# A hybrid decoder step on one core: shorter routing chain, thinned layer-norm sums, and pooling products evicted by ScalarE

## The reference

```
h = rmsnorm(x) ; p = h @ w_in                    # columns: conv value | conv gate | pool input
a = v * sigmoid(gate); y = depthwise_conv31(a)   # 1024 channels
yc = silu(layernorm(y + b_dw))                   # mean and variance over the 1024 channels
s = trailing_mean(u) - u                         # windows 2, 4, 8, 16 for 4 groups of 256
yp = (s @ w_pool[g]) * pool_scale
x = x + concat(yc, yp) @ w_out
h2 = rmsnorm(x); group = argmax(h2 @ w_rg); two best of its 8 experts by h2 @ w_re
x = x + sum_e gate_e * (silu(h2 @ w_gate[e]) * (h2 @ w_up[e])) @ w_down[e]   # 32 experts, width 512
y = rmsnorm(x)
```

## Time and profile before

| what | value |
|---|---|
| median of 3 runs | 1390.73 us (1390.59 to 1391.2) |
| profiled execution, its own time | 1391.43 us |
| its span, first to last instruction | 1389.6 us |
| granted TensorE clock, mean | 0.974 |
| PE busy | 1281.5 us (92%) |
| DVE busy | 344.3 us (25%) |
| ACT busy | 101.4 us (7%) |
| POOL busy | 102.4 us (7%) |
| data moved | 464.61 MB, mean 334 GB/s |

### The profile page before, as it was taken

The page is one execution under the profiler, slowest core; times in us unless marked ns, Lnnn a source line. Parts: engine busy times, 40 slices in busy tenths (PEclk is TensorE's granted clock), DMA queues, the critical chain, the costliest instruction groups (busy, mean ns, idle before and its releaser), DMA issues.

```text
span 1389.6 us, 16405 instructions
## 1 busy us (share of the span) xinstructions
PE 1281.5 (92%) x6548; PEld 721.1 (52%) x6548; DVE 344.3 (25%) x699; ACT 101.4 (7%) x232; POOL 102.4 (7%) x164
## 2 busy tenths in 40 slices
PE   9999989999999998989998989899889989889876
PEld 7777767777865443444343445444344444334321
DVE  4499933011342110101101011110101101010226
ACT  2100012000100000000000000000000000000012
POOL 2211152000000000000000000000000000000000
PEclk9999999999999999999999999999999999999997
DMA  9444325565439999999999999999999999999894
GB/s 237 165 143 158 122 67 170 199 243 211 166 138 372 426 426 427 428 430 425 428 426 426 428 427 427 427 425 428 421 427 422 418 427 419 428 426 410 341 321 118
DMA packets 82486, 464.61 MB, mean 334 GB/s; under 512 B 8079, under 2 KB 50191, under 8 KB 56195
## 3 DMA queue, kind: packets, MB, share of 16 engines
q1 hardware_dynamic: 76784, 455.89, 81.3%
q0 software_dynamic: 5392, 7.86, 1.8%
q10 hardware_dynamic: 283, 0.48, 0.1%
HBM read 456.67 MB, written 20.80 MB: 344 GB/s over the span
## 4 chain that ended last, share of the span: by engine, by line
PE 44%; DMA 41%; issue 7%; DVE 5%; SPq 1%; ACT 0%; DVEq 0%; ACTq 0%
DMA arena<-in_w_up_dram 41%; PE bank L716 21%; PE bank L562 14%; PE bank L737 3%; DVE arena L979 3%; PE bank L694 2%; SPq L394 1%; PE bank L788 1%; PE bank L629 1%; PE bank L646 0%; PE bank L599 0%; PE bank L511 0%; PE bank L643 0%; PE bank L791 0%; DVE arena L985 0%
## 5 line engine op out<-in xcount | busy, mean ns | idle before, releaser
L716 PE MATMUL bank<-arena,stage 128*64 128x512 f32 x1920 | 442.8, 615 | 58.3 <-DMA arena<-in_w_up_dram 58.3
L716 PEld LDWEIGHTS bank<-arena,stage 128*64 128x64 f32 x1920 | 146.0, 142 | 347.6 <-issue 304.7
L562 PE MATMUL bank<-arena,stage 128*128 128x288 f32 x1280 | 315.0, 407 | 0.8 <-DVE arena L962 0.8
L562 PEld LDWEIGHTS bank<-arena,stage 128*128 128x128 f32 x1280 | 241.9, 190 | 66.3 <-issue 0.9
L694 PEld LDWEIGHTS bank<-x1w,x1r 96*128 96x128 f32 x1536 | 174.0, 192 | 26.0 <-issue 26.0
L694 PE MATMUL bank<-x1w,x1r 96*128 96x128 f32 x1536 | 180.2, 277 | 0.0
L1222 DVE TENSOR_TENSOR a_sb<-sl_sb,bank 128x256 f32<-128x256 f32 x32 | 19.3, 604 | 498.1 <-ACT sl_sb L895 498.1
L737 PE MATMUL bank<-arena,aT 128*64 128x512 f32 x512 | 113.4, 595 | 8.5 <-ACT aT L897 8.5
L979 DVE SCALAR_TENSOR_TENSOR arena<-arena,wdw 128x256 f32<-128x256 f32 x240 | 103.0, 503 | 0.0
L1359 POOL DMA_INDIRECT expert_rows<-ysb,cur_d x31 | 30.3, 978 | 855.9 <-DVE ysb L1236 827.8
L1236 DVE TENSOR_SCALAR ysb<-bank,wslot 128x512 f32<-128x512 f32 x31 | 23.3, 751 | 255.6 <-PE bank L737 255.6
(11 more groups left out here) (232 smaller groups left out, 483.8 us busy)
## 6 DMA issues: line engine op xcount, KB each, us to landing
arena<-in_w_gate_dram SPq DMA_DIRECT2D x48, 2048.0 KB, 13.7
arena<-in_w_up_dram SPq DMA_DIRECT2D x48, 2048.0 KB, 21.1
arena<-in_w_down_dram SPq DMA_DIRECT2D x30, 2048.0 KB, 17.9
xT<-in_w_down_dram SPq DMA_DIRECT2D x15, 2048.0 KB, 20.4
stage<-in_w_down_dram SPq DMA_DIRECT2D x15, 2048.0 KB, 21.7
arena<-in_w_gate_dram SPq DMA_DIRECT2D x16, 1536.0 KB, 14.8
arena<-in_w_up_dram SPq DMA_DIRECT2D x16, 1536.0 KB, 21.1
stage<-in_w_in_dram SPq DMA_DIRECT2D x11, 2048.0 KB, 8.2
```

What stands on the lines that cost most here:

```text
L562: last = pe.matmul(ps[bank][:, 0:NTOK], wsl[a][:, k, cc * P:(cc + 1) * P], rhs[:, k, :], start=(n == 0), stop=(n == KT - 1))
L716: mm = pe.matmul(ps[4 + s][BLK * h:BLK * (h + 1), :], xgT[:, k, BLK * s:BLK * (s + 1)], w[:, :, 256 * h:256 * (h + 1)], start=(k == 0), st ...
```

## The change

- The 8-tile channel sums are thinned: VectorE first adds tiles to two (for the sum: 8 to 4 to 2; for the squares the same), PE then multiplies only two. The sum's matmuls move behind `pool_inputs(2)`, those of the squares behind `pool_inputs(3)`.
- The state transposes of the pooling rows go to banks 2 and 3, the pool products to banks 4 and 5; ScalarE evicts the products, ahead of the Silus, and then loads the Silu table by a dummy activation. `pool_line(6)` and `(7)` move ahead.
- PE waits for all eight evictions before the projection; the first dense takes the pooled half first and then waits for the convolution half.
- The last group's row squares are split: columns of tiles 0 to 2, then tile 3, before whose transposes PE waits for the first squares. The Sqrt table is loaded ahead. ScalarE, not VectorE, copies the last rows.
- `one_hot(0)` is six comparisons of 128 elements that multiply by the inverse root in the same instruction, and one addition.
- Dummies: 30 and 12 instead of 40 and 18. In the first pair, selections 2 and 3 come after the second gate/up quarter.

```diff
-AWAKE_ROUTE = (40, 18)
+AWAKE_ROUTE = (30, 12)
...
+            def channel_sum(bank, parts):
+
+                for j in range(2):
+                    last = pe.matmul(ps[bank][:, 0:NTOK], ones[:, :], parts[:, j, :], start=(j == 0), stop=(j == 1))
+                return last
...
-            pe.wait_ge(conv_chain, 4 * PERC)
-            for j in range(CT):
-                last = pe.matmul(ps[4][:, 0:NTOK], ones[:, :], yc[:, j, :], start=(j == 0), stop=(j == CT - 1))
-            last.then_inc(sum_mm, 1)
             pool_inputs(2)
+            pe.wait_ge(sum_ready, 1)
+            channel_sum(4, sqw[:, 4:6, :]).then_inc(sum_mm, 1)
+            pool_inputs(3)
             pe.wait_ge(sq_ready, 1)
-            for j in range(CT):
-                last = pe.matmul(ps[5][:, 0:NTOK], ones[:, :], sqw[:, j, :], start=(j == 0), stop=(j == CT - 1))
-            last.then_inc(sumsq_mm, 1)
-            pool_inputs(3)
+            channel_sum(5, sqw[:, 0:2, :]).then_inc(sumsq_mm, 1)
...
-                    last = pe.matmul(ps[6 + i % 2][:, 0:NTOK], wsl[0][:, 2 * g + a, dd * P:(dd + 1) * P], sT[:, 2 * g + a, :],
+                    last = pe.matmul(ps[4 + i % 2][:, 0:NTOK], wsl[0][:, 2 * g + a, dd * P:(dd + 1) * P], sT[:, 2 * g + a, :],
...
-            pe.wait_ge(st_ready, 4)
-            pe.wait_ge(mix_ready, CT)
-            pe.wait_ge(wrs_ready, 1)
-            pe.wait_ge(var_ready, 1)
+            pe.wait_ge(wp_ready, CT)
+            pooled_first = tuple(range(CT, KT)) + tuple(range(CT))
...
-                    dense(q % 2, a, q % 2, mixT, late=(wp_ready, CT) if first and q == 0 else None).then_inc(o_mm, 1)
+                    if first and q == 0:
+                        dense(q % 2, a, q % 2, mixT, order=pooled_first, late=(mix_ready, CT)).then_inc(o_mm, 1)
...
                     elif first:
+                        pe.wait_ge(st_ready, 4)
+                        pe.wait_ge(wrs_ready, 1)
...
+            pe.wait_ge(act_chain, 4 * TT)
             rows_and_router(3, 3)
...
-                            for b in ((0, 1), (2,), (3,), ())[c]:
+                            for b in ((0, 1), (), (2, 3), ())[c]:
...
+            for i in range(CT):
+                act.wait_ge(wp_mm, i + 1)
+                j = CT - 2 - 2 * (i // 2) + i % 2
+                act.activation(mixT[:, CT + j, :], ps[4 + i % 2][:, 0:NTOK], ACT.Copy, scale=pps[:, j:j + 1]).then_inc(wp_ready, 1)
+            act.activation(silu_table[:, :], ones[:, 0:1], ACT.Silu)
...
+            with act.Fori(0, 3) as o:
+                row_squares(o, 0, 4, o)
+            row_squares(3, 0, 3, 3)
+            row_squares(3, 3, 4, 4)
             act.wait_ge(act_in, 2)
             act.activation(sq[:, :], va[:, :], ACT.Sqrt).then_inc(sqrt_done, 1)
+            for t in range(TT):
+                act.copy(x1p[:, t, 96:128, :], ps[2 + t][0:TR, :].rearrange("r (p k) -> r p k", k=KT)).then_inc(row_evac, 1)
...
+            dve.wait_ge(conv_chain, 4 * PERC)
+            dve.tensor_tensor(sqw[:, 0:4, :], yc[:, 0:4, :], yc[:, 4:8, :], ALU.add).then_inc(half_sum, 1)
+            dve.wait_ge(half_sum, 1)
+            dve.tensor_tensor(sqw[:, 4:6, :], sqw[:, 0:2, :], sqw[:, 2:4, :], ALU.add).then_inc(sum_ready, 1)
             dve.wait_ge(nmean_ready, 1)
...
+            dve.wait_ge(squared, 1)
+            dve.tensor_tensor(sqw[:, 0:4, :], sqw[:, 0:4, :], sqw[:, 4:8, :], ALU.add).then_inc(half_sq, 1)
+            dve.wait_ge(half_sq, 1)
+            dve.tensor_tensor(sqw[:, 0:2, :], sqw[:, 0:2, :], sqw[:, 2:4, :], ALU.add).then_inc(sq_ready, 1)
...
-            rows(3)
...
+                if isinstance(m, int) and m == 0:
+                    for c, dst in ((0, hot0), (1, hot)):
+                        for t in range(TT):
+                            ins = dve.tensor_scalar(dst[:, t, :], iof[:, 0:P], slot[:, c, t:t + 1], rs[:, t:t + 1], ALU.is_equal, ALU.mult)
+                        ins.then_inc(hot_chain, 1)
+                    dve.wait_ge(hot_chain, 2)
+                    dve.tensor_tensor(hot, hot, hot0, ALU.add).then_inc(hot_ready, 1)
```

More of the change, by code:

```diff
@@ L141, in hybrid_decoder_step @@
         a_sb = sb("a_sb", [P, 256])
+        silu_table = sb("silu_table", [P, 1])
         sl_sb = sb("sl_sb", [P, 256])
@@ L144, in hybrid_decoder_step @@
         ss = sb("ss", [TR, TT])
-        ssp = sb("ssp", [TR, TT * 4])
+        ssp = sb("ssp", [TR, TT * 5])
+        preload = sb("preload", [TR, 1])
         va = sb("va", [TR, TT])
@@ L312, in hybrid_decoder_step @@
         sqrt_done = sem("sqrt_done")
+        squared = sem("squared")
         nmean_ready = sem("nmean_ready")
@@ L330, in hybrid_decoder_step @@
         centred = sem("centred")
+        half_sum = sem("half_sum")
+        sum_ready = sem("sum_ready")
+        half_sq = sem("half_sq")
         var_ready = sem("var_ready")
@@ L617, in _ @@
                 for j in range(4 * b, 4 * b + 4):
-                    last = pe.transpose(ps[b][0:UK, (j % 4) * P:(j % 4 + 1) * P], uk[:, j, :], ident[:, :])
+                    last = pe.transpose(ps[2 + b][0:UK, (j % 4) * P:(j % 4 + 1) * P], uk[:, j, :], ident[:, :])
                 last.then_inc(st_mm, 1)
             pe.wait_ge(slot_in[0], 16 * 7)
-            pe.wait_ge(st_ready, 2)
+            pe.wait_ge(nmean_ready, 1)
+            pe.wait_ge(var_ready, 1)
             for i in range(CT):
@@ L653, in projection @@
                         pe.wait_ge(slot_in[a], 16 * o + (16 * 7 if a else 16 * 8))
-                    dense(q % 2, a, q % 2, mixT, late=(wp_ready, CT) if first and q == 0 else None).then_inc(o_mm, 1)
+                    if first and q == 0:
+                        dense(q % 2, a, q % 2, mixT, order=pooled_first, late=(mix_ready, CT)).then_inc(o_mm, 1)
+                    else:
+                        dense(q % 2, a, q % 2, mixT).then_inc(o_mm, 1)
                     if q:
@@ L848, in pool_line @@
                          ps[c][:, SEQ:NTOK].rearrange("p (s t) -> p s t", s=NSEQ)).then_inc(u_evac[c // 2], 1)
-            for n in range(4):
+            for n in range(6):
                 pool_line(n)
@@ L854, in _ @@
             act.wait_ge(centred, 1)
[L855 to L858, removed]
+            act.activation(words(arena, O_AW, CT * NTOK), words(arena, O_YC, CT * NTOK), ACT.Square).then_inc(squared, 1)
+            pool_line(6)
+            pool_line(7)
             act.wait_ge(var_ready, 1)
             act.activation(lnr[:, :], lnv[:, :], ACT.Sqrt).then_inc(sqrt_done, 1)
-            pool_line(6)
+            for i in range(CT):
[3 more added lines that the diff above has]
+            act.activation(silu_table[:, :], ones[:, 0:1], ACT.Silu)
             act.wait_ge(yn_ready, 1)
@@ L864, in _ @@
                 act.activation(mixT[:, j, :], yc[:, j, :], ACT.Silu, bias=plb[:, j:j + 1], scale=plg[:, j:j + 1]).then_inc(mix_ready, 1)
-            pool_line(7)
-            for n, (b, r) in enumerate(((6, AK), (7, AK), (0, UK), (1, UK))):
+            for n, (b, r) in enumerate(((6, AK), (7, AK), (2, UK), (3, UK))):
                 act.wait_ge(st_mm, n + 1)
@@ L874, in _, with row_squares @@
             act.dma_start(pool_s[0, :, HP - SLEN:HP, :], strow[HP:UK, 1, :]).then_inc(st_out, 16)
-            with act.Fori(0, 4) as o:
-                act.wait_ge(row_mm, 4 * o + 4)
+            act.activation(preload[:, :], ones[0:TR, 0:1], ACT.Sqrt)
+            def row_squares(o, q0, q1, col):
+                act.wait_ge(row_mm, 4 * o + q1)
                 for t in range(TT):
-                    act.activation(ysb[0:TR, t % 2, (t // 2) * 512:(t // 2 + 1) * 512], ps[2 + t][0:TR, :], ACT.Square,
-                                   accum_out=dyn(ssp, 4 * t + o, 1, TR)).then_inc(act_chain, 1)
+                    act.activation(ysb[0:TR, t % 2, (t // 2) * 512 + q0 * P:(t // 2) * 512 + q1 * P], ps[2 + t][0:TR, q0 * P:q1 * P], ACT.Square,
+                                   accum_out=dyn(ssp, 5 * t + col, 1, TR)).then_inc(act_chain, 1)
+            with act.Fori(0, 3) as o:
+                row_squares(o, 0, 4, o)
+            row_squares(3, 0, 3, 3)
+            row_squares(3, 3, 4, 4)
             act.wait_ge(act_in, 2)
             act.activation(sq[:, :], va[:, :], ACT.Sqrt).then_inc(sqrt_done, 1)
+            for t in range(TT):
+                act.copy(x1p[:, t, 96:128, :], ps[2 + t][0:TR, :].rearrange("r (p k) -> r p k", k=KT)).then_inc(row_evac, 1)
             act.wait_ge(act_in, 3)
@@ L1006, in _ @@
             last.then_inc(wrs_ready, 1)
[L1008 to L1011, removed]
             dve.sem_inc(row_evac, 1)
@@ L1029, in _ @@
             residual(3)
-            dve.wait_ge(act_chain, 4 * TT)
+            dve.wait_ge(act_chain, 5 * TT)
             link(dve.tensor_reduce(ss[:, :], ssp3, AXX, ALU.add))
             dve.tensor_scalar(va[:, :], ss[:, :], 1.0 / D, EPS, ALU.mult, ALU.add).then_inc(act_in, 1)
-            rows(3)
             dve.wait_ge(act_in, 2)
@@ L1085, in one_hot @@
                     dve.wait_ge(key_ready, m)
```

(6 more changed lines are left out.)

1 line of the change is left out of this document (removed).

## The result

| | before | after |
|---|---|---|
| median | 1390.66 us (4 runs) | 1379.14 us (1378.88 to 1379.88, 4 runs) |
| ratio after/before | | 0.992 (95%: 0.9908 to 0.9932) |
| profiled execution / span | 1391.43 / 1389.6 us | 1379.88 / 1378.1 us |

Faster by 11.5 us where 16.4 were forecast: 1379.14 lies just above the range of 1371 to 1379. The way was right, the size was not.

The account below looks back on a forecast made before the run. The expert-weight DMA stream bounds the second half, so it must start earlier: 11.9 us before the second dense plus 4.5 in routing, 16.4 off 1391.43, gives 1375.0 (median 1374.3); range 1372 to 1377, with rivals (1) and (2) 1371 to 1379.

Parts of the forecast that it names:

- GpSimd's last group: Last pooling sums and differences before the projection: 4.6 us from 210.9, ready at 215.6, before PE asks at 218.9.
- the mix wait: PE's wait within the first dense, after its pooled half, for ScalarE's Silus of the convolution half: 1.8 us.
- the routing: Last rows, one-hot and dummies up to the first selection: selection starts 4.5 us earlier, bounds 4.1 to 4.8.
- carrying over: Microseconds saved before the load of the sixth `gu_used` (440.02 us) reach the end one to one.
- The two additions: VectorE's thinning before each channel sum: 2.1 us, at most 2.5 for the first pair, hidden from PE.
- the wait and the sums: PE before the projection: 6.29 us of convolution wait, 5.12 of sums and 2.91 of squares saved, 14.3 together.
- the wait for the last one: PE's new wait before the first dense for ScalarE's last eviction of pool products: 0.6 us lost.
- leaving a drain out of the sum: ScalarE's Silu table switch counted without the skill's drain of some 1380 ns; with it the result would be 1375.7.
- One-hot: Before the first selection: six instructions at 0.21 us and one addition take 1.9 us, against 2.20 before.
- Rival (1): PE's clock falls in the routing after a new 1.2 us wait, slowing the dummies: 1375.7 to 1377 us; chance 0.17.
- Rivals (3): In the expert stage the weight stream starts earlier but PE cannot follow it, up to 1396 us; chance 0.04.
- (4): The shift is not carried to the end because the stream's start hangs on something fixed: 1378.8 to 1390.7; chance 0.06.

Follow-up runs that it names:

- the hold: Changed kernel with VectorE's last layer-norm product waiting until GpSimd has written its last pooled differences; 1376.24 us, ratio 0.9903.
- the routing part alone: Kernel before with only the last-rows, one-hot, dummies and selection-order changes, layer norm and pooling as before; 1386.73 us, ratio 0.9973.
- the last experiment: GpSimd's trailing sums start before VectorE's convolution ends, against the changed kernel with held product, early Silu table, unsplit squares, old one-hot; 1372.94 us.

## Why the prediction was wrong

- **The step that failed** is "GpSimd's last group, 4.6 us once `pool_line(7)` is done at 210.9, is ready at 215.6, asked for at 218.9". I took GpSimd's durations from rows in which VectorE stood or only evicted from the banks, and set them beside additions that VectorE had not had. `pool_line(7)` did not release it: the chain of waits of the changed kernel runs through GpSimd without a gap from 184.74, GpSimd took up the last group only at 214.25, and it was ready at 221.5. Of these 5.9 us, 3.3 are the later start and 2.6 the subtractions held up by VectorE's product. Cost in the changed kernel: 2.8 us of waiting, shown by the hold (2.79 to 0.37), and up to 1.7 us by the clock behind it. The two halves of the first dense took 4.15 us each where I had 3.88, the mix wait was 0.3 shorter: that makes up, within 0.1 us, the 4.6 by which the second dense is later than forecast.
- The whole account: 4.6 us missing at the second dense, 1.5 in the routing (3.0 for 4.5) and 1.4 in the second expert are 7.5; 2.6 came back later, and 16.4 became 11.5. That the total fell only 4.9 us short is in part luck, as the bullet on carrying over says.
- The two additions, for which I put at most 2.5 us a pair, took 3.4 and 4.7 us. They stayed hidden from PE, as forecast, but not from GpSimd. The trace of before had the sign: centring took 2.92 us beside GpSimd and the like product 2.56 alone. I used it as a bound for VectorE and never asked what GpSimd paid. Its price stands in the same trace: one instruction of 30 elements took 2.44 us beside the centring, and 0.25 in the changed kernel, where it ran alone.

```profile
191.64 2.44 POOL L1345 TENSOR_TENSOR arena<-arena,rcol 128x30 f32<-128x30 f32 x1
```

- As forecast: the wait and the sums (PE at 193.60 and 210.09, forecast 193.7 and 210.3), the eviction (0.50 us, all eight at that), the wait for the last one (0.59; 0.6), the mix wait (1.51; 1.8), the w_out slice in time. The dummy Silu starts 0.01 us behind its table load (225.75 and 1.28 long, then 227.04), so leaving a drain out of the sum was right.
- Last rows: the split ends the squares 3.0 us behind tile 2's transposes, 2.74 before: 0.3 us lost where I said 0.2. Logits 9.25 us earlier, 1.9 of them by the moved copies; forecast 2.0.
- One-hot: six instructions at 0.27 us each make it 2.2 us long. My 0.21 was worked out from 96 elements with a single pointer; the 0.3 us did not come.
- Rival (1), the clock in the routing, came in three of eight profiles with the wait of 1.14 us, the two of the changed kernel among them, and cost about 1 us there. I gave it 0.17.
- Carrying over: the load of the sixth `gu_used` came 8.9 us earlier, the end of the span 11.5. Of the 2.6 us between, 1.7 is the last waiting products' slow pace in the profile of before, and so chance: they took 7.09 us in nine of the thirteen profiles and 8.41 to 9.96 in four. From that load to the end the thirteen profiles show 946.8 to 948.0 us once those products' excess over 7.09 is taken off: the shift is carried one to one within a microsecond. Rivals (3) and (4) are out.
- Selections behind quarter 1: the load for the second `gu_used` goes out 2.9 us sooner against the selection and nothing later moves, as said: from selection to the sixth, 48.6 us before and 48.4 with the routing part alone.

On the lock itself, the Trainium skill says under "SBUF — State Buffer", Who interferes with whom, that a VectorE instruction with two SBUF inputs contends with a GpSimd instruction that reads SBUF. With that the forecast would have been better; the trace agrees with it (0.48 us of subtractions took 3.07 beside the product). Of VectorE's two-port modes the same section of the Trainium skill says that whoever issues first has the shared pair for the whole instruction. If one carries that over to instructions with two inputs, the last experiment does not bear it out: GpSimd's sums were under way from 163.97 on, and the taps, which ran until 182.35, took 25.74 us all the same.

Still open: what decides whether the clock falls behind one and the same wait, and why the second expert's products are slow in six profiles. The runs show that the clock falls in some executions and not in others, and no run told them apart. These places are worth 1 to 1.7 us each, as much as several of the differences between the experiments' times.

## What to carry to other kernels

Work moved onto VectorE "in the shadow" has to be priced for GpSimd too: if its instructions read two operands from SBUF, lay GpSimd's timeline beside them and follow GpSimd to whoever waits for it. The cure was a single wait, on the engine that had time (VectorE, whose product nobody needed yet). An engine that stands in a queue of evictions is the place for a table load, and what is worth taking from a chain of small instructions is the large copy in its middle, not the split at its start.

## What the runs showed of the hardware

- GpSimd's 128x32 subtractions, 0.48 us alone, took 3.07 us beside a 128x2304 product of VectorE; its four 128x844 additions took 6.9 us alone, 8.49 beside VectorE's two additions and 26.14 when they were started under its taps, which stayed at 25.74.
- VectorE's single instructions suffer as well: 2.70 us for 1152 elements against 1.36, and 1.17 to 1.43 us for steps of 288 elements against 0.46.
- ScalarE's eviction of 128x288 with a scale pointer takes 0.50 us, and brings no table back.
- After the same wait of 2.7 to 2.8 us the next eight instructions took 2.21 us in two profiles and 3.61 to 3.88 in three; after a wait of 1.14 us the next 60 dummies took 6.94 us in five and 8.5 in three.
